# Attention of a two-layer decoder: suffix products that accumulate on the negated scores in PSUM

## The reference

```python
z = jnp.einsum("bhqd,bhkd->bhqk", q[:, :, t0:n_keys], k[:, :, :n_keys]).astype(jnp.float32) * scale
strict = s_pos < t_pos
log_keep = jnp.where(strict, jax.nn.log_sigmoid(-z), 0.0)
log_keep_after = lax.cumsum(log_keep, axis=3, reverse=True) - log_keep
weight = jnp.where(strict, jnp.exp(jax.nn.log_sigmoid(z) + log_keep_after), 0.0)
out_blocks.append(jnp.einsum("bhqk,bhkd->bhqd", weight.astype(v.dtype), v[:, :, :n_keys]))
```

## Time and profile before

| | |
|---|---|
| time, median of 3 runs | 1506.68 us (1504.1 to 1507.3) |
| profiled execution: its own time, its span | the span, first to last instruction, is 1504.8 us; no other time is given for it |
| busy in the span | TensorE 90%, VectorE 45%, ScalarE 35%, GpSimd 2% |
| mean granted clock of TensorE | 0.963 of full speed |
| moved by DMA | 474.31 MB, mean 315 GB/s |
| chain that ended last | TensorE 67%, DMA 14%, SyncE's queue 11%, VectorE 4% |
| attention stage | 491.2 to 537.9 us |

### The profile page before, as it was taken

How to read it: one execution, slowest core, us unless ns; L and a number is a source line. 1 busy time by engine, 2 the same in 40 slices (tenths; PEclk the granted TensorE clock), 3 DMA queues, 4 the chain that set the end, 5 groups by cost and what they waited for, 6 DMA issues and landing times.

```text
span 1504.8 us, 25408 instructions
## 1 busy us (share of the span) xinstructions
PE 1353.3 (90%) x11187; PEld 970.9 (65%) x11188; DVE 681.9 (45%) x762; ACT 525.5 (35%) x582; POOL 36.0 (2%) x66
## 2 busy tenths in 40 slices
PE   3999999999999788999999999999898888987776
PEld 2764678888789546777676777676675665643332
DVE  5943444454443626755454755454664453100002
ACT  2323433434243613544343444343453442000001
POOL 3000000000000002000000000000000000000000
PEclk9979999999999997999999999999998999999999
DMA  8883895545485114679999979999989999999994
GB/s 289 315 311 141 311 358 203 187 168 197 175 332 190 57 56 168 225 293 411 411 412 412 402 301 411 411 412 412 404 333 412 413 412 410 411 412 413 412 413 192
DMA packets 206793, 474.31 MB, mean 315 GB/s; under 512 B 9986, under 2 KB 10030, under 8 KB 206670
## 3 DMA queue, kind: packets, MB, share of 16 engines
q1 hardware_dynamic: 199968, 470.83, 80.8%
q10 hardware_dynamic: 6702, 1.71, 0.5%
HBM read 471.47 MB, written 1.05 MB: 314 GB/s over the span
## 4 chain that ended last, share of the span: by engine, by line
PE 67%; DMA 14%; SPq 11%; DVE 4%; issue 2%; ACT 1%; ACTq 1%; POOL 0%; POOLq 0%; DVEq 0%
PE ps L2369 39%; DMA ring<-in_moe_w_down_dram 11%; SPq L508 11%; PE ps L2679 7%; PE ps L2691 5%; DMA ring<-in_ada_w_dram 2%; PE ps L2345 2%; PE ps L2540 2%; PE ps L2180 2%; PE ps L2244 1%; DVE arena L1298 1%; PE ps L2634 1%; PE ps L2671 1%; PE ps L2510 1%; PE ps L2305 1%
## 5 line engine op out<-in xcount | busy, mean ns | idle before, releaser
L1932 DVE TENSOR_TENSOR ring_lo<-ring,w 128x2048 fp32r<-128x2048 f32 x126 | 288.1, 2289 | 186.2 <-ACT w L1069 150.0
L1069 ACT ACTIVATE w<-ring 128x2048 fp32r<-128x2048 f32 x126 | 240.4, 1912 | 223.8 <-PE ps L2369 207.7
L2679 PE MATMUL ps<-ring,arena 128*32 128x128 f32 (+1 forms) x5376 | 242.6, 294 | 30.1 <-DMA ring<-in_moe_w_gate_up_dram 23.0
L2679 PEld LDWEIGHTS ps<-ring,arena 128*32 128x32 f32 (+1 forms) x5376 | 185.5, 115 | 90.1 <-DMA ring<-in_moe_w_gate_up_dram 32.6
L2369 PE MATMUL ps<-ring_lo,x_hi 128*128 128x512 f32 x592 | 230.9, 390 | 0.0
L2369 PE MATMUL ps<-w,x_hi 128*128 128x512 f32 x336 | 135.3, 403 | 4.4 <-DVE ring_lo L1932 2.6
L1547 DVE TENSOR_TENSOR ring_lo<-ring,w_hi 128x2048 fp32r<-128x2048 f32 x42 | 95.6, 2290 | 85.6 <-ACT w_hi L785 85.6
L2369 PE MATMUL ps<-w,x_lo 128*128 128x512 f32 x336 | 131.2, 390 | 0.0
L2369 PEld LDWEIGHTS ps<-ring_lo,x_hi 128*128 128x128 f32 x592 | 111.3, 188 | 21.2
L2691 PE MATMUL ps<-ring,tri 128*32 128x512 f32 (+1 forms) x448 | 73.8, 673 | 36.6 <-DMA ring<-in_moe_w_down_dram 34.6
L785 ACT ACTIVATE w_hi<-ring 128x2048 fp32r<-128x2048 f32 x42 | 78.8, 1909 | 49.1 <-PE ps L2369 42.1
(11 more groups left out here) (401 smaller groups left out, 1719.2 us busy)
## 6 DMA issues: line engine op xcount, KB each, us to landing
ring<-in_moe_w_gate_up_dram SPq DMA_DIRECT2D x112, 2048.0 KB, 17.8
ring<-in_moe_w_down_dram SPq DMA_DIRECT2D x56, 2048.0 KB, 18.3
ring<-in_ada_w_dram SPq DMA_DIRECT2D x24, 2048.0 KB, 10.8
ring<-in_ffn_w_gate_up_dram SPq DMA_DIRECT2D x14, 2048.0 KB, 11.9
ring<-in_ffn_w_down_dram SPq DMA_DIRECT2D x7, 2048.0 KB, 7.8
ring<-in_sb_w_qkv_dram SPq DMA_DIRECT2D x6, 2048.0 KB, 9.2
ring<-in_s_w_out_dram SPq DMA_DIRECT2D x2, 2048.0 KB, 8.3
ring<-in_sb_w_out_dram SPq DMA_DIRECT2D x2, 2048.0 KB, 14.1
```

Source lines behind the costliest of these rows:

```text
L1069: act.activation(half3(h).bitcast(F32R), ff_half(gran(pair_place(*main_granule(n))), half), ACT.Copy).then_inc(whi_done, 1)
L1932: dve.tensor_tensor(ff_half(ring_lo[place % RING][:, :], half).bitcast(F32R), ff_half(gran(place), half), half3(h), ALU.subtract).then_inc ...
L2679: ins = pe.matmul(dst[width * r:width * r + width, 0:cols], x[:, k, 0:width], weights[:, k, cols * r:cols * r + cols], start=k == 0, stop= ...
```

## The change

The scale of the queries is negated, so the scores in PSUM are -z. The three bank pairs 0 and 1, 2 and 3, 4 and 5 are given to the pairs of heads in turn (`head_banks`). The suffix products are accumulated onto the scores in the same banks, so that a bank holds suffix - z, and the second Exp reads the bank with a scale of -1. This removes ScalarE's copy of the scores and VectorE's argument step. Abs is one ScalarE instruction over both heads, out of PSUM. Softplus is (ln(...)) - min(-z, 0), read out of PSUM. The output copy moves from ScalarE to VectorE. The order of TensorE's stages is unchanged; within `scores` the two heads of one block of columns follow one another, and `scores(h)` waits for the second Exp of `h-3`.

```diff
...
+        def head_banks(h):
+
+            return ps[:, 2 * (h % 3):2 * (h % 3) + 2, 0:384]
         block = ctx.enter_context(nc.Block())
@@ -930,7 +933,7 @@
                 wait_used(act, N_QKV + r)
                 base = 0 if r % 2 else Y_BANK
                 act.activation((qT if r < 2 else kT)[:, 4 * (r % 2):4 * (r % 2) + 4, :], ps[:, base:base + 4, 0:256],
-                               ACT.Copy, scale=DH ** -0.5 if r < 2 else 1.0).then_inc(qk_done, 1)
+                               ACT.Copy, scale=-DH ** -0.5 if r < 2 else 1.0).then_inc(qk_done, 1)
 
             for h in range(2, 12):
                 q_round(h)
@@ -939,31 +942,22 @@
                 if h == 2:
                     act.preload_act_table_set("natural_log_exp_and_others")
 
-            def o_out(h):
-                act.wait_ge(o_ps, h + 1)
-                act.activation(oT[:, h, :], ps[:, 6 + h % 2, 0:256], ACT.Copy).then_inc(o_done, 1)
-
             for h in range(HEADS // 2 + 1):
                 b = h % 2
                 if h < HEADS // 2:
                     act.wait_ge(z_ps, h + 1)
-                    if h >= 3:
-                        act.wait_ge(o_ps, h - 2)
-                    act.activation(z_w[:, h % 3], ps[:, 2 * b:2 * b + 2, 0:384], ACT.Copy).then_inc(zcopy_done, 1)
                     if h >= 2:
                         act.wait_ge(sp_done, h - 1)
-                    act.activation(z_e[:, b, 0], ps[:, 2 * b, 0:384], ACT.Abs).then_inc(zsize_done, 1)
+                    act.activation(z_e[:, b], head_banks(h), ACT.Abs).then_inc(zsize_done, 1)
                     act.wait_ge(zsize_done, h + 1)
-                    act.wait_ge(zabs_done, h + 1)
                     act.activation(z_e[:, b], z_e[:, b], ACT.Exp, scale=-1.0).then_inc(exp_done, 1)
                     act.wait_ge(exp_done, h + 1)
                     act.activation(z_e[:, b], z_e[:, b], ACT.Ln, bias=1.0).then_inc(ln_done, 1)
                 if h:
-                    act.wait_ge(arg_done, h)
-                    act.activation(z_w[:, (h - 1) % 3], z_w[:, (h - 1) % 3], ACT.Exp).then_inc(wexp_done, 1)
-                if h >= 2:
-                    o_out(h - 2)
-            o_out(HEADS // 2 - 1)
+                    act.wait_ge(sfx_ps, h)
+                    if h >= 4:
+                        act.wait_ge(o_ps, h - 3)
+                    act.activation(z_w[:, (h - 1) % 3], head_banks(h - 1), ACT.Exp, scale=-1.0).then_inc(wexp_done, 1)
             wait_used(act, N_SBOUT + 1)
             y_stats(2, y_banks)
             ada_part(10)
@@ -1638,39 +1632,31 @@
 
             mask = strict[:, :].unsqueeze(1).unsqueeze(1).to_broadcast([P, 2, 2, P])
 
-            def size(h):
-
-                z = z_w[:, h % 3]
-                dve.wait_ge(zcopy_done, h + 1)
-                if h >= 2:
-                    dve.wait_ge(sp_done, h - 1)
-                stt(z_e[:, h % 2, 1], z[:, 1], -1.0, z[:, 1], ALU.mult, ALU.max).then_inc(zabs_done, 1)
-
-            size(0)
+            def o_out(h):
+
+                dve.wait_ge(o_ps, h + 1)
+                dve.tensor_copy(oT[:, h, :], ps[:, 6 + h % 2, 0:256]).then_inc(o_done, 1)
+
             for h in range(HEADS // 2 + 1):
                 if h < HEADS // 2:
                     b = h % 2
-                    z = z_w[:, h % 3]
                     dve.wait_ge(ln_done, h + 1)
                     if h >= 2:
                         dve.wait_ge(sfx_ps, h - 1)
 
-                    stt(z_p[:, b], z, 0.0, z_e[:, b], ALU.max, ALU.add).then_inc(sp_done, 1)
+                    dve.scalar_tensor_tensor(out=z_p[:, b], in0=head_banks(h), scalar=0.0, in1=z_e[:, b], op0=ALU.min,
+                                             op1=ALU.subtract, reverse1=True).then_inc(sp_done, 1)
                     dve.wait_ge(sp_done, h + 1)
                     dve.tensor_tensor(on_diagonal(z_p[:, b]), on_diagonal(z_p[:, b]), mask, ALU.mult
                                       ).then_inc(spm_done, 1)
-                if h + 1 < HEADS // 2:
-                    size(h + 1)
                 if h:
                     dve.wait_ge(wexp_done, h)
                     for g in range(2):
                         w = on_diagonal(z_w[:, (h - 1) % 3])[:, g]
                         stt(w, w, 1.0, mask[:, g], ALU.min, ALU.mult).then_inc(w_done, 1)
-                if h < HEADS // 2:
-                    dve.wait_ge(sfx_ps, h + 1)
-
-                    z = z_w[:, h % 3]
-                    stt(z, ps[:, 4:6, 0:384], -1.0, z, ALU.mult, ALU.add).then_inc(arg_done, 1)
+                if h >= 2:
+                    o_out(h - 2)
+            o_out(HEADS // 2 - 1)
             gate_diag(2)
             gate_copy(2)
             wait_used(dve, N_SBOUT + 1)
@@ -2486,35 +2472,37 @@
 
             def scores(h):
 
-                b = h % 2
                 pe.wait_ge(qk_done, 4)
-                if h >= 2:
-                    pe.wait_ge(zcopy_done, h - 1)
-                    pe.wait_ge(zsize_done, h - 1)
-                for g in range(2):
-                    r = slice(DH * g, DH * g + DH)
-                    pe.matmul(ps[:, 2 * b + g, 0:256], kT[r, h, 0:P], qT[r, h, :], start=True, stop=True)
-                    ins = pe.matmul(ps[:, 2 * b + g, 256:384], kT[r, h, P:SEQ], qT[r, h, P:SEQ], start=True, stop=True)
+                if h == 2:
+                    pe.wait_ge(v_out, 4)
+                if h >= 3:
+                    pe.wait_ge(wexp_done, h - 2)
+                z = head_banks(h)
+                for keys, queries, at in ((slice(0, P), slice(0, SEQ), slice(0, 256)),
+                                          (slice(P, SEQ), slice(P, SEQ), slice(256, 384))):
+                    for g in range(2):
+                        r = slice(DH * g, DH * g + DH)
+                        ins = pe.matmul(z[:, g, at], kT[r, h, keys], qT[r, h, queries], start=at.start == 0, stop=False,
+                                        skip_group_check=True)
                 ins.then_inc(z_ps, 1)
 
             def suffix(h):
 
                 b = h % 2
                 pe.wait_ge(spm_done, h + 1)
-                if h:
-                    pe.wait_ge(arg_done, h)
-                else:
+                for g in range(2):
+                    z, y = z_p[:, b, g], head_banks(h)[:, g]
+                    pe.matmul(y[:, 0:256], incl[:, :], z[:, 0:256], start=False, stop=False, skip_group_check=True)
+                    pe.matmul(y[:, P:256], ones[:, :], z[:, 256:384], start=False, stop=False, skip_group_check=True)
+                    ins = pe.matmul(y[:, 256:384], incl[:, :], z[:, 256:384], start=False, stop=True,
+                                    skip_group_check=True)
+                ins.then_inc(sfx_ps, 1)
+
+            def values(h):
+
+                b = h % 2
+                if h == 0:
                     pe.wait_ge(v_out, 4)
-                for g in range(2):
-                    z = z_p[:, b, g]
-                    pe.matmul(ps[:, 4 + g, 0:256], incl[:, :], z[:, 0:256], start=True, stop=False)
-                    pe.matmul(ps[:, 4 + g, P:256], ones[:, :], z[:, 256:384], start=False, stop=True)
-                    ins = pe.matmul(ps[:, 4 + g, 256:384], incl[:, :], z[:, 256:384], start=True, stop=True)
-                ins.then_inc(sfx_ps, 1)
-
-            def values(h):
-
-                b = h % 2
                 pe.wait_ge(w_done, 2 * h + 2)
                 above(pe, o_done, h - 1)
                 for g in range(2):
```

More of the change, by code:

```diff
@@ L316, in program @@
             sem("q_xhi"), sem("q_xlo"), sem("q_whi"), sem("q_wlo"), sem("q_half"), sem("plain_done"))
[L317 to L321, removed]
+        z_ps, exp_done, ln_done, sp_done, spm_done = (
+            sem("z_ps"), sem("exp_done"), sem("ln_done"), sem("sp_done"), sem("spm_done"))
+        sfx_ps, wexp_done, w_done, o_ps, o_done = (
+            sem("sfx_ps"), sem("wexp_done"), sem("w_done"), sem("o_ps"), sem("o_done"))
         lg_ps, lmax_done, pexp_done, sel_done, rank_ps, route_done = (
@@ L2503, in suffix @@
                 pe.wait_ge(spm_done, h + 1)
-                if h:
-                    pe.wait_ge(arg_done, h)
-                else:
-                    pe.wait_ge(v_out, 4)
                 for g in range(2):
-                    z = z_p[:, b, g]
-                    pe.matmul(ps[:, 4 + g, 0:256], incl[:, :], z[:, 0:256], start=True, stop=False)
-                    pe.matmul(ps[:, 4 + g, P:256], ones[:, :], z[:, 256:384], start=False, stop=True)
-                    ins = pe.matmul(ps[:, 4 + g, 256:384], incl[:, :], z[:, 256:384], start=True, stop=True)
+                    z, y = z_p[:, b, g], head_banks(h)[:, g]
[3 more added lines that the diff above has]
+                                    skip_group_check=True)
                 ins.then_inc(sfx_ps, 1)
```

## The result

The changed kernel takes 1496.76 us in the median of its first 4 runs (1495.23 to 1497.91), beside 1505.39 for the kernel before (1501.57 to 1507.30, 4 runs): ratio 0.9945, 95% interval 0.9927 to 0.9963. Two further groups of runs gave 0.9919 (0.9903 to 0.9936) and 0.9919 (0.9898 to 0.9939). It is faster by 0.5 to 0.8%; forecast was 1499.7 us, which is 0.5%, in a range from 1496.6 to 1503.6. The profiled execution has a span of 1496.1 us and its own time is 1497.91.

A forecast was written before the change was run, and what follows sets the result against it. A 4.67 us per-pair loop of hand-overs through VectorE's argument step was taken to bound the attention stage. Gains of 6.4 us up to the output projection plus 0.6 there, 7.0 total, gave 1499.7 us, range 1496.6 to 1503.6.

The forecast's parts named there:

- the clock comes back sooner: Rival: only the first half of the low-clock stretch at the attention stage's start remains; gain 9.4 us, 1497.3; chance 0.22.
- the forecast case: Low-clock stretch at the stage's start stays the same, 6.0 to 7.8 us gained; chance 0.51.
- The bound: Attention stage: hand-overs through VectorE's argument step, softplus, mask and TensorE's suffix products set 4.67 us a pair of heads.
- The new loop: Attention stage without the argument step: a loop over two pairs of heads, 4.04 us a pair, saving 0.62 a pair.
- S, A, E, L, P, M, X, V: Score products, Abs, Exp, Ln, softplus, mask, suffix products, value products in turn; predicted loop 8.08 us for two pairs.
- ScalarE had room: In the new loop of the attention stage, ScalarE was said to have 0.6 us a pair to spare.
- Costs of the new operations: Attention stage: Abs 0.81 us, last Exp out of PSUM 0.82, softplus out of PSUM 0.96, output copy on VectorE 0.41.
- The start and the low clock: Stage start, up to the score products of pair 3: gain 1.43 us, with the low clock in the same place.
- I count half, 0.6: First output projection matmuls: 1.4 us lost to a low clock behind TensorE's pause may not come; 0.6 us counted as gain.
- nothing arrives at the end: Rival: expert loads behind the stage set the time and are not moved by attention; gain lost, 1506.5 us; chance 0.08.
- Slower: Rival: TensorE stays at 1.2 GHz through all of the attention stage, which ends at about 545; 1514 us; chance 0.02.

The follow-up runs named there:

- the kernel before with the filling: Eight matmuls that nobody reads added in TensorE's first wait of the stage, against the kernel before: 1503.98 us, ratio 0.9985.

## Why the prediction was right

- **How right.** The time came out 2.9 us below the forecast, 0.2 inside the range, and the median of all 14 runs (1495.3) lies below the range. That the first four fell inside it is in part luck of the draw: the profiled one of them took 1497.91, 1.15 above their median. The number is nearer to the rival "the clock comes back sooner" (1497.3) than to the forecast case. The mechanism, the loop, is what held.
- **The bound**: a loop of hand-overs through the argument step. Shown by putting the step back, alone: 4.66 us a pair again.
- **The new loop**, 8.08 us for two pairs through S, A, E, L, P, M, X, V: measured 8.07. That it is this loop is shown from two sides: 0.71 added inside it on ScalarE gives 8.76, and V taken out of it gives 7.26 (there TensorE's own work, twice 3.61 to 3.65, is as long, so this side alone would not prove the length). That ScalarE had room does not help a step inside the loop.
- **Costs of the new operations**: within 0.02 us each. The Trainium skill's page "VectorE: DVE Perf Modes", section "The TRN2 errata", has fixed costs from which 0.065 us more follows for VectorE out of PSUM, an estimate. That does not fit here: L1647 takes 958 ns, L1298 from SBUF 949 (0.01, as the earlier trace rows had it).
- **The start and the low clock.** From the first S to S of pair 3 the forecast has 13.73 us, the first profile 12.48; from there to S of pair 7 16.16 against 16.13, and on to the projection 10.42 against 10.43. So all that the stage gained beyond the forecast (7.68 against 6.4) lies in its start, where the low stretch was 3.4 us long and not 6.8. With the long one (third profile) the start takes 13.53 and the stage 40.09, 6.6 less than 46.72: the forecast's own case, to 0.2. The mechanism of the rival "the clock comes back sooner" occurred, but not through the change: the length varies between executions, in both kernels. The Trainium skill's page "TensorE: Matmul & The Clock Gate" says in Part 1 that the point at which the clock changes depends on phase and varies between runs. The profiles agree that it varies (39.04, 39.04, 40.09 after; 46.72, 46.74, 47.17 before); that phase is the reason, no run here shows.
- **The end: the term that was mis-sized.** "I count half, 0.6", of 1.4 us. The 1.4 compared the first 16 records with a third of the next 48 (6.87), but at full clock they take 7.13. So only 1.14 us went to the low clock, and all of it came back; by the second and third profiles it is 1.1 and 1.7. In nine profiles of kernels without the argument step there was no low clock at the end of the stage, in four of five with it there was. Two waits of TensorE there are longer with the step, ahead of the last X and ahead of the last V (in brackets; before, then after):

```profile
531.59 0.70 PE L2510 MATMUL ps<-arena,tri 128*128 128x256 f32 x2 [1.83 <-DVE arena L1660]
...
536.33 0.69 PE L2523 MATMUL ps<-arena 128*64 128x256 f32 x4 [1.91 <-DVE arena L1298]
```

```profile
525.52 0.70 PE L2495 MATMUL ps<-arena,tri 128*128 128x256 f32 x2 [0.78 <-DVE arena L1650]
...
529.24 0.66 PE L2511 MATMUL ps<-arena 128*64 128x256 f32 x4 [0.89 <-DVE arena L1292]
```

The prediction named the second. The first fits as well: in the third profile of the kernel before (531.33) and in the one with the argument step put back (528.09) a low clock began within 0.7 us of the start of the last X, ahead of the last V's wait. And the kernel before with the filling has both waits and no low clock at its end. Which wait counts, or whether it is TensorE's denser work (84% against 72%), is open; no run changed one alone.

- **What arrives.** Nothing was lost to the loads: over 14 profiles the rest from the start of the projection's last record is 934.5 to 937.0 us, with stages from 35.8 to 47.3. The rival "nothing arrives at the end" fell.
- **Slower**: the low clock did not stay; from 503 to 531 it was 1.00.
- **What stays open.** The profiles explain 8.8 us. All medians together, 42 runs before (1505.9) and 14 after (1495.3), differ by 10.6. The part ahead of the stage is the same program in all kernels and took 487.4 to 493.0 us in 14 profiles; I take the other 1.8 us for its scatter. In the three profiles of each kernel, 2.0 us of the spans' mean difference (10.8) indeed lie ahead of the stage; over all five profiles with the argument step and all nine without it the part ahead differs by only 0.4 (491.1 and 490.7). That this is the whole of the 1.8 is not shown. No run took the bank pairs or the score order back inside the new loop, so what they are worth there is open too.

## What to carry to other kernels

When several engines are each busy some 70%, write down the loop of starts, and then also the next loop, which closes over two turns because of the order in which one engine is programmed: it said both what the change brings and which further edit pays (score products ahead of value products, 1.6 us of the stage). A step that is removed from beside the loop is worth nothing, and in the new loop it may be worth something. Where a stage is 3% of the program and the rest scatters by 5 us, read the stage from profiles, several of them, and let the medians only confirm the sign.

## What the runs showed of the hardware

- The same wait of TensorE ahead of the first suffix products (5.30 us from first S to first X) was followed by a low clock 3.4 us long in some executions (stage 39.04) and 6.8 in others (40.09). Eight matmuls in that wait kept the clock at 1.00 in all three profiles of the changed kernel's versions with them; the stage was 1.6 us shorter than with the short stretch. In the kernel before, the same matmuls kept it at 1.00 only up to 503.78, and then it was low for 3.4 us.
- Matmuls that add onto the scores in the bank, in place of starting a sum of their own, take the same time: by the first records of the timeline X to V is 1.95 us, as before.
- The part of the program ahead of the stage, unchanged in all kernels, varied by 5.6 us between executions.
